# Attention of a two-block transformer kernel: heads handled one at a time, and in pairs that share the array

## The chip, the cores and the metric

The kernel runs on one core of a Trainium2 chip. The metric is the device time of one execution in microseconds. Before the change it is 2275.27 us, the median of three runs (2274.09 to 2283.27 us). The profile shown below is of a further execution of the same program.

## The reference

One sequence of 512 tokens, 1024 features wide, goes through two transformer blocks in float32. The change touches only the attention of the first one. All its heads have 64 features (`HEAD_DIM`), and a query attends to keys at or before it.

```
# first block, 8 NSA heads in 2 groups of 4, 8 DSA heads on one key head
s = einsum('bgrqd,bsgd->bgrqs', qb, kk) * scale       # window and selected branch: a key head per group
p = masked_softmax(s, mask); o = einsum('bgrqs,bsgd->bgrqd', p, vv)
o = g[..., 0:1] * o_cmp + g[..., 1:2] * o_slc + g[..., 2:3] * o_win
# DSA: the 128 best keys of each query by an index score, then the same softmax attention
score = where(key_pos <= tq, einsum('bqh,bqhs->bqs', w, relu(logits)), -inf); _, sel = top_k(score, 128)
o = concatenate([o_nsa, o_dsa], -1) @ w_out;  x = x + gt1 * rms_norm(o, g_post_mix)
```

At 512 tokens all selected blocks and the whole window lie within reach, so the selected and the window branch are plain causal attention with keys of their own. The compressed branch attends to 31 keys, each made from 32 tokens by a small two-layer network.

## The kernel before, in words

Everything is laid out with features on the partitions and tokens along the row. Each engine has one instruction stream, written out by hand, and semaphores tie the streams together. Nothing plans them: the order in the code is the order on the engine. `claim(bank, sem, value)` makes TensorE wait until the last reader of a PSUM bank is done.

The first block computes 16 projection tiles, then the attention in question, then the `w_out` product and the feed-forward layers. The second block follows. The attention is a loop over 96 jobs, `jobs = [(t, br, hh)]` (L268): `t` is one of four tiles of 128 queries, `br` is the branch (0 selected, 1 window, 2 DSA) and `hh` the head. A job of tile `t` sees `kv = (t+1) * 128` keys. Its steps are

- `qk` (L468), TensorE: scores into bank `j % 3`. A head has 64 features, so this matmul uses 64 of the 128 rows of the array.
- `masked` (L1392), VectorE: adds the mask to the negated scores, writes `sneg` in SBUF and takes the row's minimum.
- `Exp` (L986), ScalarE: from `sneg` into `prob`, with the row's sum.
- `scaled` (L1402), VectorE: reciprocal of the sum, then `prob` times it and the gate.
- `turn_probs` (L477), TensorE: `t+1` transposes of 128x128 into bank 3 or 4; `probs_turned` (L969), ScalarE: copies them to `probT`.
- `pv` (L485), TensorE: `t+1` matmuls, 64 columns of the array wide, into half of the partitions of bank 5 (NSA) or 6 (DSA).

In step `j` TensorE issues `qk(j)`, `turn_probs(j-2)` and `pv(j-3)`; VectorE `masked(j)` and `scaled(j-1)`; ScalarE the `Exp` of `j` and the copy of `j-2`. Other work is put between the jobs. TensorE has `ada_cols(2)` at job 2, `compress(0)` and `compress(1)` (L425, 32 matmuls each over weights that arrive in three tiles of the four-slot ring) at jobs 5 and 9, and `cmp_keys` at 14. The compressed branch of each tile has `cmp_scores` (L501), four jobs later `cmp_turn`, and seven jobs later `cmp_out`, which adds into bank 5. They use bank 7. VectorE has the 32 remaining rounds of the top-128 search (`top_round`, L1342: a `MAX8` and a match-replace over 384 or 512 scores), `late_mods`, its part of the compressed branch, and `outputs` (L1416), which splits a finished output bank into high and low parts for `w_out`. It also makes the low part of the first three `w_out` tiles (L1229) at job 31.

A float32 matmul shows as two records of TensorE in the trace, a transpose as one.

Of the kernel before, what the change touches and what calls it, by code (L numbers as in the profile page):

```python
# [10 lines left out]
ALU = mybir.AluOpType  # L11
# [3 lines left out]
P = 128  # L15
T = 512
# [120 lines left out]
def build(nc, xt, consts, cols, pos, ada, ada_late, mats, extra, out):  # L137
    ctx = ExitStack()
    with ctx:
# [38 lines left out]
        smin, _ = at("smin", [P, 3])  # L178
# [89 lines left out]
        jobs = [(t, br, hh) for t in range(NT) for br in range(3) for hh in range(HEADS)]  # L268
# [3 lines left out]
        CMP_AT = [16] + [24 * t for t in range(1, NT)]  # L272
# [13 lines left out]
        def _(pe):  # L286
# [181 lines left out]
            def qk(j):  # L468
                t, br, hh = jobs[j]
                kv = (t + 1) * P  # L470
                b = 64 * (hh // 4) if br < 2 else 64 * (hh % 2)
                q = QN + hh % 4 if br < 2 else QD + hh // 2
                claim(j % 3, "smin", j + 1)
                pe.matmul(bank[:, j % 3, 0:kv], proj[b:b + DH, q, t * P:(t + 1) * P],  # L474
                          proj[b:b + DH, (KSL, KW, KDD)[br], 0:kv], start=True, stop=True).then_inc(S("scores"), 1)

            def turn_probs(j):  # L477
                pe.wait_ge(S("probs_scaled"), j + 1)
                claim(3 + j % 2, "probT", j + 1)
                for i in range(jobs[j][0] + 1):  # L480
                    mm = pe.transpose(bank[:, 3 + j % 2, i * P:(i + 1) * P], prob[j % 4][:, i * P:(i + 1) * P],  # L481
                                      const("ident"))
                mm.then_inc(S("probs_turned"), 1)

            def pv(j):  # L485
                t, br, hh = jobs[j]
                vc = ((hh // 4) * DH, P + (hh // 4) * DH, 2 * P)[br]
                pe.wait_ge(S("probT"), j + 1)

                half = br // 2  # L490
                if hh == 0 and br != 1:
                    claim(5 + half, "oT", 2 * t + half + 1)
                b, c = DH * (hh % 2), hh // 2
                for i in range(t + 1):

                    mm = pe.matmul(bank[b:b + DH, 5 + half, c * P:(c + 1) * P], vtok[:, i, vc:vc + DH],  # L496
                                   probT[j % 4][:, i * P:(i + 1) * P], start=(i == 0 and hh < 2 and br != 1),
                                   stop=False, skip_group_check=True)
                mm.then_inc(S("pv"), 1)
# [22 lines left out]
            def cmp_out(t):  # L522
                pe.wait_ge(S("cmp_probT"), t + 1)
                for g in range(2):
                    for c in range(2):
                        pe.matmul(bank[:, 5, (2 * g + c) * P:(2 * g + c + 1) * P], vcmp[:, g, c * P:(c + 1) * P],
                                  cpt[:, g, :], start=False, stop=False, skip_group_check=True)

            pe.wait_ge(S("roped"), 16)
            n = len(jobs)  # L530
            for j in range(n + 3):
                if j < n:
                    qk(j)
                    if j == 2:
# [5 lines left out]
                    if j == 14:  # L540
                        cmp_keys()
                    if j in CMP_AT:
                        if j == CMP_AT[0]:
                            pe.wait_ge(S("cmp_kv"), 1)
                        cmp_scores(CMP_AT.index(j))
                    if j - 4 in CMP_AT:
                        cmp_turn(CMP_AT.index(j - 4))
                    if j - 7 in CMP_AT:
                        cmp_out(CMP_AT.index(j - 7))
                if 2 <= j < n + 2:  # L550
                    turn_probs(j - 2)
                if 3 <= j:
                    pv(j - 3)
# [299 lines left out]
        def _(act):  # L853
# [115 lines left out]
            def probs_turned(j):  # L969
                kv = (jobs[j][0] + 1) * P  # L970
                act.wait_ge(S("probs_turned"), j + 1)
                if j >= 4:
                    act.wait_ge(S("pv"), j - 3)
                act.activation(probT[j % 4][:, 0:kv], bank[:, 3 + j % 2, 0:kv], ACT.Copy).then_inc(S("probT"), 1)

            def outputs(t, half):
                act.wait_ge(S("pv"), 24 * t + 16 + 8 * half)
# [3 lines left out]
            for j, (t, br, hh) in enumerate(jobs):  # L981
                kv = (t + 1) * P
                act.wait_ge(S("smin"), j + 1)
                if j >= 4:
                    act.wait_ge(S("probs_turned"), j - 3)
                act.activation(prob[j % 4][:, 0:kv], sneg[j % 3][:, 0:kv], ACT.Exp, scale=-1.0,  # L986
                               bias=smin[:, j % 3:j % 3 + 1], accum_out=ssum[:, j % 4:j % 4 + 1])\
                   .then_inc(S("probs"), 1)
                if j in CMP_AT:
# [910 lines left out]
```

## Time and profile before

| | us |
|---|---|
| median of three runs | 2275.27 |
| the profiled execution, whole | 2262.76 |
| its span, first to last instruction | 2261.0 |
| TensorE matmul busy in the span | 2118.5 (94%) |
| TensorE weight load busy | 1613.5 (71%) |
| VectorE busy | 974.3 (43%) |
| ScalarE busy | 709.2 (31%) |

Busy time is time in which an instruction of that engine was running. The weight loads run beside the matmuls. The mean granted TensorE clock was 0.942 of full speed. The attention loop lies at 194 to 474 us of the span.

### The profile page before, as it was taken

The numbers are of one execution on the slowest core, as the hardware profiler recorded it, in microseconds if no ns is written. First come the engines' busy times: TensorE is split into PE (matmuls) and PEld (weight loads), VectorE is DVE, ScalarE is ACT, GpSimd is POOL, SyncE is SP. The second block draws the span as 40 slices with busy tenths as digits, with TensorE's granted clock in tenths as the row PEclk, the third lists the DMA queues.
The fourth block names the chain that finished last, engine by engine and source line by source line (L and its number), as shares of the span: only waits on it lengthen the run. The fifth ranks groups of instructions, "written<-read, shape, count | busy, mean of one in ns | idle before, by whom it ended". The sixth has DMA issues, their size and how long they took to land. (4 is left out here: it accounts for less than half of the span.)

```text
span 2261.0 us, 25224 instructions
## 1 busy us (share of the span) xinstructions
PE 2118.5 (94%) x10170; PEld 1613.5 (71%) x10170; DVE 974.3 (43%) x1654; ACT 709.2 (31%) x1163; POOL 124.7 (6%) x94
## 2 busy tenths in 40 slices
PE   5999999998999999999999989995898889999999
PEld 3666655575888887688888766663777767888887
DVE  4454587536443444533233423337544454332332
ACT  3321244434232333322223244546111133321221
POOL 0002000010000001000000102332000001000000
PEclk9997568999999999999999999997999999999999
DMA  8542000011222222123223121110000012232231
GB/s 334 186 158 105 28 29 1 1 47 56 94 95 97 97 94 93 56 99 107 84 93 121 57 75 57 47 38 0 1 1 1 2 56 84 93 115 75 99 118 50
DMA packets 41587, 172.14 MB, mean 76 GB/s; under 512 B 4609, under 2 KB 4865, under 8 KB 38145
## 3 DMA queue, kind: packets, MB, share of 16 engines
q1 hardware_dynamic: 41472, 170.54, 21.8%
q8 instruction: 81, 1.33, 0.2%
q14 instruction: 34, 0.27, 0.0%
HBM read 168.43 MB, written 2.10 MB: 75 GB/s over the span
## 5 line engine op out<-in xcount | busy, mean ns | idle before, releaser
L312 PE MATMUL bank<-hs,wsp 128*128 128x512 f32 x1392 | 554.0, 398 | 20.7 <-DVE hs L1268 11.5
L313 PE MATMUL bank<-hs,wsp 128*128 128x512 f32 x1392 | 545.9, 392 | 0.0
L314 PE MATMUL bank<-hs,wsp 128*128 128x512 f32 x1392 | 545.6, 392 | 0.0
L878 ACT ACTIVATE wsp<-ring 128x1024 fp32r<-128x1024 f32 (+2 forms) x244 | 268.8, 1104 | 851.8 <-PE bank L314 850.4
L1229 DVE TENSOR_TENSOR wsp<-ring,wsp 128x1024 fp32r<-128x1024 f32 (+2 forms) x244 | 312.0, 1281 | 383.2 <-ACT wsp L878 382.7
L312 PEld LDWEIGHTS bank<-hs,wsp 128*128 128x128 f32 x1392 | 263.9, 190 | 100.5 <-issue 38.7
L313 PEld LDWEIGHTS bank<-hs,wsp 128*128 128x128 f32 x1392 | 264.2, 190 | 55.7 <-issue 1.9
L314 PEld LDWEIGHTS bank<-hs,wsp 128*128 128x128 f32 x1392 | 263.8, 189 | 55.7
L314 PE MATMUL bank<-hids,wsp 128*128 128x512 f32 x608 | 241.0, 396 | 0.0
L313 PE MATMUL bank<-hids,wsp 128*128 128x512 f32 x608 | 241.0, 396 | 0.0
L312 PE MATMUL bank<-hids,wsp 128*128 128x512 f32 x608 | 241.0, 396 | 0.0
L313 PEld LDWEIGHTS bank<-hids,wsp 128*128 128x128 f32 x608 | 114.5, 188 | 27.9
L314 PEld LDWEIGHTS bank<-hids,wsp 128*128 128x128 f32 x608 | 114.5, 188 | 27.9
L312 PEld LDWEIGHTS bank<-hids,wsp 128*128 128x128 f32 x608 | 114.5, 188 | 27.9
L1739 POOL TENSOR_TENSOR arena<-arena 128x512 f32<-128x512 f32 x24 | 43.2, 1799 | 1382.2 <-ACT arena L890 1382.2
L1537 DVE SCALAR_TENSOR_TENSOR x<-bank,x 128x512 f32<-128x512 f32 x40 | 27.7, 692 | 174.8 <-PE bank L314 174.8
L474 PE MATMUL bank<-arena 64*128 64x128 f32 (+3 forms) x192 | 96.4, 594 | 3.0 <-DVE arena L1320 3.0
L986 ACT ACTIVATE arena<-arena,smin 128x128 f32<-128x128 f32 (+3 forms) x96 | 53.9, 561 | 128.8 <-DVE smin L1399 128.4
L496 PE MATMUL bank<-tmp,arena 128*64 128x128 f32 x480 | 88.9, 325 | 0.0
L1527 DVE TENSOR_TENSOR tmp<-tmp,bank 128x512 f32<-128x512 f32 x44 | 30.3, 688 | 128.5 <-PE bank L314 128.5
L496 PEld LDWEIGHTS bank<-tmp,arena 128*64 128x64 f32 x480 | 59.2, 159 | 20.8 <-issue 18.3
L481 PEld LDWEIGHTS bank<-cst,arena 128*128 128x128 f32 x240 | 30.0, 159 | 52.7 <-issue 32.4
(276 smaller groups left out, 2213.5 us busy)
## 6 DMA issues: line engine op xcount, KB each, us to landing
ring<-m_gate SPq DMA_DIRECT2D x44, 512.0 KB, 3.3
ring<-m_up SPq DMA_DIRECT2D x44, 512.0 KB, 3.3
ring<-m_down SPq DMA_DIRECT2D x32, 704.0 KB, 4.0
ring<-m_w_in SPq DMA_DIRECT2D x38, 512.0 KB, 3.4
arena<-ada_late SPq DMA_DIRECT2D x16, 1024.0 KB, 4.8
ring<-m_w_up SPq DMA_DIRECT2D x32, 512.0 KB, 3.3
ring<-m_w_down SPq DMA_DIRECT2D x32, 512.0 KB, 3.2
ring<-m_w_out SPq DMA_DIRECT2D x16, 512.0 KB, 3.4
```

Source lines behind the costliest of these rows:

```text
L312: pe.matmul(out, lhs[0], rhs[0], start=start, stop=False)
L313: pe.matmul(out, lhs[0], rhs[1], start=False, stop=False)
L314: return pe.matmul(out, lhs[1], rhs[0], start=False, stop=stop)
L474: pe.matmul(bank[:, j % 3, 0:kv], proj[b:b + DH, q, t * P:(t + 1) * P], proj[b:b + DH, (KSL, KW, KDD)[br], 0:kv], start=True, stop=True).t ...
L481: mm = pe.transpose(bank[:, 3 + j % 2, i * P:(i + 1) * P], prob[j % 4][:, i * P:(i + 1) * P], const("ident"))
L496: mm = pe.matmul(bank[b:b + DH, 5 + half, c * P:(c + 1) * P], vtok[:, i, vc:vc + DH], probT[j % 4][:, i * P:(i + 1) * P], start=(i == 0 an ...
L878: act.activation(wsp[:, s % SPLIT, 0, 0:size], ring[:, i % RING, 0:size], ACT.Copy)\
L986: act.activation(prob[j % 4][:, 0:kv], sneg[j % 3][:, 0:kv], ACT.Exp, scale=-1.0, bias=smin[:, j % 3:j % 3 + 1], accum_out=ssum[:, j % 4:j ...
L1229: dve.tensor_tensor(wsp[:, s % SPLIT, 1, 0:size], ring[:, i % RING, 0:size], wsp[:, s % SPLIT, 0, 0:size].bitcast(F32), ALU.subtract).then ...
L1527: dve.tensor_tensor(f, f, bank[:, 2 * (nn % 2) + 1, :], ALU.mult).then_inc(S("gated"), 1)
L1537: dve.scalar_tensor_tensor(out=x[:, nn, :], in0=bank[:, nn % 4, :], scalar=scale, in1=x[:, nn, :], op0=ALU.mult, op1=ALU.add).then_inc(S(" ...
L1739: pool.tensor_tensor(sq[:, 0, :], sq[:, 0, :], sq[:, k, :], ALU.add).then_inc(S("sq_sum"), 1)
```

## The change

The 96 jobs become 48 pairs of heads, `pairs = [(t, br, i)]`. The two heads of a pair lie in different row halves of the array for `qk` (partitions 0 to 63 and 64 to 127 of `proj`) and in different column halves for `pv`. For the NSA branches a pair is head `i` and head `i + 4`, one of each group; for DSA heads `2i` and `2i + 1`. Each step now issues both heads' `qk`, into two of four score banks, then both heads' transposes, then the `pv` matmuls alternately. Transposed probabilities go to banks 4 and 7, one bank for both heads while `t < 2` and one bank each after. `sneg` and `prob` are replaced by five pair buffers `soft`, in which mask, `Exp` and scaling work in place. One reciprocal serves both heads. The other work is put at the pair that corresponds to its old job or close to it, and the top-128 rounds go one to a pair from pair 4 to pair 35. The rows of `w_out` are reordered on the host to match.

```diff
-        sneg = [area(at * K, (T,)) for at in (66, 68, 70)]
-        prob = [area(at * K, (T,)) for at in (10, 12, 14, 16)]
-        probT = [tmp[:, at, :] for at in (2, 3, 4, 5)]
+        soft = [area(at * K, (2, T)) for at in (66, 70, 0, 10, 14)]
+        probT = [tmp[:, 2 + 2 * n:4 + 2 * n, :] for n in range(2)]
...
+        pairs = [(t, br, i) for t in range(NT) for br in range(3) for i in range(4)]
+        NP = len(pairs)
+        turned_at = list(itertools.accumulate(1 if t < 2 else 2 for t, br, i in pairs))
...
-        CMP_AT = [16] + [24 * t for t in range(1, NT)]
+        CMP_AT = [8] + [12 * t for t in range(1, NT)]
+        CMP_OUT_AT = [11] + [12 * t + 4 for t in range(1, NT)]
...
+            def qk(p):
+                t, br, i = pairs[p]
                 kv = (t + 1) * P
+                for e in range(2):
+                    b = 2 * (p % 2) + e
+                    claim(b, "smin", 2 * p + e + 1)
+                    pe.matmul(bank[:, b, 0:kv], proj[DH * e:DH * e + DH, (QN, QN, QD)[br] + i, t * P:(t + 1) * P],
+                              proj[DH * e:DH * e + DH, (KSL, KW, KDD)[br], 0:kv], start=True, stop=True)\
+                      .then_inc(S("scores"), 1)
+            def turn_probs(p):
+                t = pairs[p][0]
+                for e in range(2):
+                    if t < 2:
+                        b, c = (4, 7)[p % 2], 2 * e
...
+                    else:
+                        b, c = (4, 7)[e], 0
+                        claim(b, "probT", turned_at[p] - 1 + e)
+                    pe.wait_ge(S("probs_scaled"), 2 * p + e + 1)
+                    for k in range(t + 1):
+                        mm = pe.transpose(bank[:, b, (c + k) * P:(c + k + 1) * P], soft[p % 5][:, e, k * P:(k + 1) * P],
+                                          const("ident"))
...
+            def pv(p):
...
+                for k in range(t + 1):
+                    for e in range(2):
+                        vc = (e * DH, P + e * DH, 2 * P)[br]
+                        mm = pe.matmul(bank[DH * e:DH * e + DH, 5 + half, i * P:(i + 1) * P], vtok[:, k, vc:vc + DH],
+                                       probT[p % 2][:, e, k * P:(k + 1) * P], start=(k == 0 and i == 0 and br != 1),
+                                       stop=False, skip_group_check=True)
...
-                    if j == 5:
+                    if p == 2:
                         compress(0)
-                    if j == 9:
+                    if p == 4:
                         compress(1)
...
+            def probs_turned(p):                      # ScalarE
...
+                if p >= 2:
+                    act.wait_ge(S("pv"), p - 1)
+                if t < 2:
+                    act.wait_ge(S("probs_turned"), turned_at[p])
+                    act.activation(probT[p % 2][:, :, 0:kv],
+                                   bank[:, (4, 7)[p % 2], :].rearrange("p (e k) -> p e k", e=2)[:, :, 0:kv],
+                                   ACT.Copy).then_inc(S("probT"), 1)
...
+            def masked(p, e):                         # VectorE
...
+                if p >= 5:
+                    dve.wait_ge(S("probs_turned"), turned_at[p - 5])
...
+            def scaled(p):
+                t, br, i = pairs[p]
+                n = 2 * (p % 2)
+                dve.wait_ge(S("probs"), 2 * p + 2)
+                do(dve.reciprocal(rsum[:, n:n + 2], ssum[:, n:n + 2]))
+                for e in range(2):
+                    v, r = soft[p % 5][:, e, 0:(t + 1) * P], rsum[:, n + e:n + e + 1]
...
+            for p in range(NP + 1):
+                if p < NP:
+                    masked(p, 0)
+                    masked(p, 1)
...
+                if p >= 1:
+                    scaled(p - 1)
...
-                if rounds < 3 * ROUNDS and j < n and j >= (8, 8, 24)[rounds // ROUNDS] + 2 * (rounds % ROUNDS):
+                if rounds < 3 * ROUNDS and p >= 4 + rounds - ROUNDS:
                     top_round(rounds)
...
+    w_out = f["w_out"][0]
+    paired = w_out[0:512].reshape(2, 4, DH, D).transpose(1, 0, 2, 3).reshape(512, D)
```

## Rows read from the trace of the kernel before

**Rows 1.** Windows, tiles 0 to 3: busy PE, PEld, DVE, ACT, POOL, PEclk, DMA share, GB/s.

```profile
194.00:271.00 77.00, 73.20 (x293) 55.86 (x294) 32.05 (x142) 18.91 (x74) 0.00 (x0) 0.52 0.13 47
271.00:334.00 63.00, 60.35 (x212) 34.98 (x212) 50.76 (x162) 25.70 (x80) 0.00 (x0) 0.64 0.08 26
334.00:398.00 64.00, 63.80 (x285) 38.01 (x284) 42.33 (x133) 27.16 (x76) 0.00 (x0) 0.82 0.00 1
398.00:474.00 76.00, 74.53 (x387) 45.31 (x386) 37.58 (x111) 34.48 (x79) 0.00 (x0) 0.93 0.00 1
```

**Rows 2.** Waits at 194 to 474 us: waiter, releaser, us in total, times, longest.

```profile
DVE arena L1399 <- PE bank L474: 83.2, 49, 14.6
...
DVE arena L1427 <- PE bank L505: 10.4, 4, 3.2
```

**Rows 3.** Timeline of TensorE, one job of tile 3: start, us, line, records.

```profile
441.81 1.12 PE L474 MATMUL bank<-arena 64*128 64x512 f32 x2
442.86 0.66 PE L481 MATMUL bank<-cst,arena 128*128 128x128 f32 x4
443.45 1.09 PE L496 MATMUL bank<-tmp,arena 128*64 128x128 f32 x8
444.47 0.69 PE L474 MATMUL bank<-arena 64*128 64x512 f32 x1
```

**Rows 4.** Timeline of TensorE, one job of tile 1 at the low clock.

```profile
320.09 1.22 PE L474 MATMUL bank<-arena 64*128 64x256 f32 x2
321.24 0.69 PE L481 MATMUL bank<-cst,arena 128*128 128x128 f32 x2
321.86 1.12 PE L496 MATMUL bank<-tmp,arena 128*64 128x128 f32 x4
322.90 1.22 PE L474 MATMUL bank<-arena 64*128 64x256 f32 x2
```

**Rows 5.** Timeline of TensorE at 103.2 to 103.3 us, two index heads.

```profile
103.24 0.49 PE L422 MATMUL bank<-arena 64*128 64x256 f32 x2
```

**Rows 6.** Timeline of TensorE at 103.8 to 104.8 us, four column tiles of 32.

```profile
103.87 1.06 PE L374 MATMUL bank<-arena,c 128*32 128x512 f32 x8
```

**Rows 7.** Timeline of TensorE, `qk` of one job of tile 1, full clock.

```profile
304.31 0.70 PE L474 MATMUL bank<-arena 64*128 64x256 f32 x2
304.94 0.44 PE L481 MATMUL bank<-cst,arena 128*128 128x128 f32 x2
```

**Rows 8.** Timeline of TensorE in the second block, column halves, full clock.

```profile
1735.98 0.45 PE L792 MATMUL bank<-arena,wal 128*64 128x128 f32 x4
1736.25 0.40 PE L794 MATMUL bank<-arena 128*64 128x128 f32 x4
```

**Rows 9.** VectorE's groups by shape, 194 to 474 us: busy us, mean ns, idle before.

```profile
L1399 DVE CUSTOM_DVE_ANT_0 arena<-bank,cst 128x512 f32<-128x512 f32 x16 | 11.1, 691 | 20.5 <-PE bank L474 20.5
...
L1411 DVE TENSOR_SCALAR arena<-arena,rsum,gates 128x512 f32<-128x512 f32 x16 | 8.7, 547 | 0.6
...
L1399 DVE CUSTOM_DVE_ANT_0 arena<-bank,cst 128x128 f32<-128x128 f32 x24 | 6.9, 291 | 36.5 <-PE bank L474 35.7 <-DVE arena L1347 0.4
...
L1411 DVE TENSOR_SCALAR arena<-arena,rsum,gates 128x128 f32<-128x128 f32 x16 | 5.5, 346 | 0.6
```

**Rows 10.** VectorE's groups, shapes together, the same stretch.

```profile
L1346 DVE MAX8 best<-arena 128x8 f32<-128x384 f32 (+1 forms) x32 | 19.9, 620 | 0.0
L1347 DVE MATCH_REPLACE8 arena<-best,arena 128x384 f32<-128x384 f32 (+1 forms) x32 | 19.5, 609 | 0.0
L1408 DVE RECIPROCAL rsum<-ssum 128x1 f32<-128x1 f32 x96 | 15.3, 159 | 1.2 <-ACT arena L986 0.6
```

**Rows 11.** TensorE's groups, the same stretch.

```profile
L432 PE MATMUL bank<-wal,ring 128*128 128x64 f32 x128 | 27.8, 422 | 0.0
```

**Rows 12.** The page's costliest groups, whole span.

```profile
L1229 DVE TENSOR_TENSOR wsp<-ring,wsp 128x1024 fp32r<-128x1024 f32 (+2 forms) x244 | 312.0, 1281 | 383.2 <-ACT wsp L878 382.7
```

**Rows 13.** DMA issues at 160 to 300 us: KB each, us to landing.

```profile
ring<-m_cmp1v SPq DMA_DIRECT2D x3, 704.0 KB, 5.3
```

More of the change, by code:

```diff
@@ L1 @@
+import itertools
 from contextlib import ExitStack
@@ L466, in _ @@
             late_piece(15)
-            def qk(j):
-                t, br, hh = jobs[j]
+            def qk(p):
+                t, br, i = pairs[p]
                 kv = (t + 1) * P
[L471 to L475, printed above, removed]
@@ L490, in pv @@
+            def pv(p):
+                t, br, i = pairs[p]
                 half = br // 2
-                if hh == 0 and br != 1:
+                pe.wait_ge(S("probT"), turned_at[p])
+                if i == 0 and br != 1:
                     claim(5 + half, "oT", 2 * t + half + 1)
[L493 to L498, printed above, removed]
+                for k in range(t + 1):
[4 more added lines that the diff above has]
+                                       stop=False, skip_group_check=True)
@@ L967, in _ @@
             copy_ada_rows(2)
[L969 to L974, printed above, removed]
+            def probs_turned(p):
+                t = pairs[p][0]
+                kv = (t + 1) * P
+                if p >= 2:
[5 more added lines that the diff above has]
+                                   ACT.Copy).then_inc(S("probT"), 1)
+                else:
+                    for e in range(2):
+                        act.wait_ge(S("probs_turned"), turned_at[p] - 1 + e)
+                        act.activation(probT[p % 2][:, e, 0:kv], bank[:, (4, 7)[e], 0:kv], ACT.Copy)\
+                           .then_inc(S("probT"), 1)
@@ L976, in outputs @@
             def outputs(t, half):
-                act.wait_ge(S("pv"), 24 * t + 16 + 8 * half)
+                act.wait_ge(S("pv"), 9 if t + half == 0 else 12 * t + 8 + 4 * half)
                 act.activation(hs[:, 0, 4 * half:4 * half + 4, t * P:(t + 1) * P],
                                bank[:, 5 + half, :].rearrange("p (c t) -> p c t", c=4), ACT.Copy).then_inc(S("oT_hi"), 1)
-            for j, (t, br, hh) in enumerate(jobs):
+            for p, (t, br, i) in enumerate(pairs):
                 kv = (t + 1) * P
[L983 to L989, printed above, removed]
-                    act.wait_ge(S("cmp_shift"), CMP_AT.index(j) + 1)
+                for e in range(2):
+                    n = 2 * (p % 2) + e
+                    act.wait_ge(S("smin"), 2 * p + e + 1)
+                    act.activation(soft[p % 5][:, e, 0:kv], soft[p % 5][:, e, 0:kv], ACT.Exp, scale=-1.0,
+                                   bias=smin[:, n:n + 1], accum_out=ssum[:, n:n + 1]).then_inc(S("probs"), 1)
+                if p in CMP_AT:
+                    act.wait_ge(S("cmp_shift"), CMP_AT.index(p) + 1)
@@ L1845, in lay_out @@
         mats["cmp1" + name] = np.ascontiguousarray(w1.reshape(P, 3, SLOT).transpose(1, 0, 2))
-    mats["w_out"] = tiles(f["w_out"][0])
+    w_out = f["w_out"][0]
+    paired = w_out[0:512].reshape(2, 4, DH, D).transpose(1, 0, 2, 3).reshape(512, D)
+    mats["w_out"] = tiles(np.concatenate([paired, w_out[512:]], 0))
     mats["w_up"] = tiles(f["w_up"][0])
```

146 lines of the change are left out of this document (64 added, 82 removed).

## The prediction, made before the change was run

> **What bounds the kernel now.** Busy shares of a whole span mix stages, so I began with the windows and cut the attention loop, 194 to 474 us, at its four query tiles. The matmul records of TensorE fill 272 of 280 us, VectorE is busy 163 and ScalarE 106 [rows 1]. The table of waits says the same from the other side: VectorE waited 83 us for scores [rows 2]. So TensorE sets the pace, and the loop can shrink only as far as TensorE's work does and VectorE lets it.
>
> Two things are to be seen in the rows of TensorE. First, the granted clock: 0.52, 0.64, 0.82 and 0.93 of full over the four tiles [rows 1]. The clock has two levels, 2.4 and 1.2 GHz, so (1 - share) x 2 of each window passed at the lower: 74, 45, 23 and 11 us, about 153 of the 280. Second, the make-up of a job. In tile 3 at full clock scores, transposes and `pv` start at 441.81, 442.86 and 443.45, and the next job at 444.47 [rows 3]: 1.05, 0.59 and 1.02 us, 2.66 together. Four more records of 128 columns make the difference between 0.59 and 1.02, so one pass of 128 columns costs 0.108 us. The job has 8 + 4 + 8 passes, 2.16 us; 0.50 us is lost at its three changes of kind. Tile 1 at the lower clock: 1.15, 0.62, 1.04, together 2.81 [rows 4]; a pass is 0.21 us (two more passes cost 0.42), the job has 4 + 2 + 4, so 2.1 us and 0.71 fixed. By the passes (5, 10, 15, 20 for tiles 0 to 3) a job costs 1.76, 2.81, 3.86, 4.91 us at the lower clock and 1.04, 1.58, 2.12, 2.66 at full; the 1.58 appears as such, from 302 to 306 us, of which the `qk` part of 0.63 is shown [rows 7].
>
> **The change, part by part.** *Do the halves of the array run together?* All hangs on it, and the trace has both kinds. Two index heads in the two row halves start both their first records within 0.1 us, two records by 103.3 [rows 5], and the whole pair over 256 keys, four records, is done when the next line starts at 103.87 [rows 6], 0.63 us. One head of tile 1 over 256 keys takes 304.31 to 304.94, also 0.63 [rows 7]. The second head was free. Column tiles: eight records of four tiles of 32 columns take 1.06 us [rows 6], where one 512-column matmul takes 1.05 [rows 3]. And two heads in the column halves with 128 rows, the very form of `pv`: four records from 1735.98 to 1736.25, 0.27 us [rows 8], where already two passes one after the other cost 0.22. So `qk` and `pv` of a pair cost what one head's do now, and the transposes, which use the whole array, double.
>
> The Trainium skill says otherwise on one point. TensorE: Matmul & The Clock Gate, Part 3 (The mechanism) has it that matmuls are "pc-monotone in start AND end — strict FIFO, no reordering". If each head's two records are issued together, by that rule the second head could not start until the first head's second record did, and a pair would cost one and a half times a head. The trace disagrees: the second record is there within 0.1 us, not after 0.3. It stands as a rival below.
>
> *TensorE per pair*: a job plus t+1 passes. At the lower clock 1.97, 3.23, 4.5, 5.75 us for tiles 0 to 3; at full clock 1.15, 1.8, 2.44, 3.09. Two jobs now: 5.32 in tile 3 at full clock, 4.24 in tile 2, 5.62 in tile 1 at the lower, 3.5 in tile 0.
>
> *VectorE per pair*: the mask step 291 to 691 ns and the scaling 346 to 547 by width, evenly spaced in between (133 and 67 ns for 128 columns) [rows 9], twice each, and one reciprocal of 159 instead of two [rows 10]: 1.44, 1.83, 2.24, 2.64 us, and some 0.15 for handing over between instructions (an estimate from starts in the timeline). The search adds one round per pair at pairs 4 to 35: 620 + 609 ns and gaps [rows 10], 1.3 us. With it: 2.9 in tile 0, 3.3 in tile 1, 3.8 to 3.9 in tile 2 (its rounds are the wide ones); 2.8 without it in tile 3. So VectorE takes over as the bound from pair 4 to somewhere in tile 2. The half of the reciprocals that goes saves 48 x 0.16 = 7.6 us of an engine that sets the pace in most of the loop; it is inside these sums. ScalarE has 34.5 us in tile 3 for 24 jobs [rows 1], 2.9 a pair, under TensorE's 3.09, and its copies for tiles 0 and 1 become one for two heads.
>
> *Depth and waits.* What is queued behind each new wait: on TensorE `turn_probs(p-2)` waits for `scaled(p-2)`, and behind it are `pv(p-3)` and `qk(p+1)`. In tile 3 counted from the start of `qk(p-1)`: scores at 1.15, two mask steps to 2.55, scaling of pair p-2 to 3.8; TensorE asks for it at 3.09 + 1.05. `pv(p-3)` needs the copies behind the two `Exp` of p-1, at about 4.6, and asks at 3.09 + 2.1. There is slack of 0.3 to 0.6 us, so the five buffers are never the limit in steady state; I count 0.06 us a pair for it, 3.15.
>
> *Moved steps.* `compress(1)` comes two pairs after `compress(0)`, 3.3 us by the prices above, where four jobs gave 7. Its last two weight tiles can only be fetched into slots that `compress(0)` frees, and land 5.3 us after issue [rows 13]: the cover is gone and TensorE waits some 2.5 us there. `cmp_scores` and its relatives keep their count. They share bank 7 with the transposes, so each tile gets a chain of scores, mask, turn and copy through that bank. VectorE waits 10.4 us in four times for `cmp_scores` already [rows 2]; with its nine short operations a tile the branch costs about 7 us a tile when VectorE is the bound. I take 7 (bounds 4, if it all lies beside TensorE, and 10). The host's reordering of `w_out` and the splits at pair 15 and 16 cost what they did, three of 1.28 us [rows 12].
>
> **The sum**, tile by tile, against 194.0 to 473.8 us of the trace, 279.8 us.
> - Tile 0, now 77.4 (271.5 less 194.0): pairs 0 to 3 at 2.0 = 8; 128 records of `compress` are 27.8 us busy at the lower clock [rows 11] and stay, 27.4; eight pairs at 2.9 = 23; the weight wait 2.5; VectorE's nine copies for the compressed keys 2.5; the branch 7; the start with `ada_cols` 1.5. Together 72.
> - Tile 1, now 62.7: TensorE 3.23 at the lower clock and VectorE 3.3 lie so close that neither covers the other's slips, 3.35 x 12 = 40; branch 7; outputs with their waits 4; `w_out` splits 3.8. Together 55.
> - Tile 2, now 63.5: VectorE alone would give 3.9, TensorE at the lower clock 4.5, at full 2.44. The present loop shows both levels in this tile [rows 1] and I expect both again, as a full-clock TensorE would stand idle 1.5 of 3.9 us and a low one not at all. 4.2 x 12 = 50; 7; 4. Together 61.
> - Tile 3, now 76.1: the search is over, TensorE is the bound at full clock: eleven steps of 3.15 = 35; 9 for the first steps (the same tile now loses 9 over eight times 2.66 there); 1 for outputs; 9 to drain three pairs and the last output. Together 54.
>
> 72 + 55 + 61 + 54 = 242, 38 us less. The profiled execution was 2262.8 us and would be 2225; the median of the runs, 12.5 us above it, goes from 2275.3 to 2237. Nothing else of the program is touched, and the `w_out` product starts behind the last output as now.
>
> **The rivals.**
> 1. *The clock stays low through tiles 2 and 3.* For it: TensorE will have idle time in tile 2 that it has not now, and low spells of 23 and 11 us are there already. Against: in tile 3 a pair at the lower clock leaves TensorE no idle time at all, and the present jobs came back from just that state. Tile 2 at 4.5 gives 65, tile 3 at 5.75 with its longer drain 90: 72 + 55 + 65 + 90 = 282, and 2277 us.
> 2. *A pair costs one and a half heads* in `qk` and `pv`. At tile 3 that adds half of 16 passes, 0.86 us, 10 us over the tile; 0.64 at full clock in tile 2, partly under VectorE, 5; 0.84 at the lower in tile 1, 9; 1 in tile 0: 25 of the 38 go, 2262 us.
> 3. *VectorE's queue and TensorE's waits add instead of overlapping*, as masks wait for scores queued behind a `pv` that waits for ScalarE. At 0.7 us a pair in tiles 1 and 2 and 0.4 in tile 3: 22 us, 2259 us. For it: 83 us of such waits now. Against: `qk` may run two pairs ahead.
> 4. *Each change of half drains the array.* Then the halves don't overlap and the alternating `pv` pays at every matmul the 0.17 us that a change of kind costs now. In tile 3 eight such changes for two, 1.0 us above two jobs, or with `qk`'s 1.2; 0.8 in tile 2, 0.5 in tile 1, 0.2 in tile 0: 12 x 2.7 = 32 us slower, 2307 us. It decides if the second half's record starts after its partner ends. The skill's TensorEngine Tiling (Array Packing), Key Properties, lets only a change of mode drain and not of tile, and here the rows side with it: four records in 0.27 us [rows 8] leave no room for a drain between them.
>
> **Chances.** Forecast 0.70, rival 3 0.12, rival 1 0.08, rival 4 0.05, rival 2 0.05. A change of 0.5%, 11 us, is about what a measurement can tell. Faster by more: the forecast, rival 3 and half of rival 2, 0.85. Within: rival 1 and half of rival 2, 0.10. Slower: rival 4, 0.05. Low end: VectorE's pace in tiles 1 and 2 with TensorE at full clock (3.3 and 3.9 a pair, 4 us less), the branch at 4 a tile (12 less), drain and start shorter (9 less): 2212. High end: past rivals 2 and 3, short of rival 1, 2268.
>
> **What would show it.** Two records of L474's successor starting together, in both the score and the `pv` lines; a pair every 3.1 us in tile 3; VectorE busy 155 to 160 us in a loop of some 242, hardly waiting for TensorE from pair 5 to tile 2; a wait of a few us before the second `compress`; the clock at its lower level in tiles 0 and 1. The forecast fails if the pair in tile 3 takes over 4 us, or if PEclk of tile 3 falls under 0.8.

## The result: 2208.22 us, faster by more than forecast

The changed kernel takes 2208.22 us (median of four runs, 2207.65 to 2210.44), beside 2274.79 for the kernel before (median of four): a ratio of 0.9701, interval 0.9677 to 0.9725. That is 66.6 us less. The forecast was 2237, 38 us less, with a range from 2212, so the direction was right and the time lies 4 us below the range. The profiled execution took 2208.48 us, its span is 2206.7 (2261.0 before).

The page of the changed kernel, whole span:

```profile
span 2206.7 us, 25046 instructions
...
PE 2030.2 (92%) x10202; PEld 1568.1 (71%) x10202; DVE 963.1 (44%) x1606; ACT 704.1 (32%) x1139; POOL 124.7 (6%) x94
...
PEclk9997589999999999999999999996999989999999
```

TensorE lost 88 us of busy time, VectorE 11. The windows of the changed kernel, tiles 0 to 3 and then two stretches of the rest, with the columns of [rows 1]:

```profile
194.00:260.50 66.50, 57.03 (x294) 47.05 (x294) 28.10 (x128) 16.78 (x62) 0.00 (x0) 0.50 0.14 54
260.50:304.00 43.50, 30.84 (x212) 18.90 (x210) 38.36 (x126) 21.89 (x63) 0.00 (x0) 0.75 0.11 37
304.00:354.00 50.00, 37.38 (x282) 23.17 (x280) 44.76 (x133) 25.33 (x72) 0.00 (x0) 0.90 0.00 1
354.00:412.50 58.50, 50.20 (x428) 33.99 (x424) 39.93 (x115) 36.12 (x86) 0.00 (x0) 0.91 0.01 2
412.80:1500.00 1087.20, 1041.83 (x4334) 808.07 (x4334) 426.11 (x533) 388.02 (x562) 99.45 (x74) 0.98 0.23 78
1500.00:2206.00 706.00, 647.97 (x3906) 530.85 (x3906) 286.85 (x404) 160.09 (x217) 10.17 (x6) 0.95 0.17 56
```

In tile 2 TensorE is busy 37 of 50 us and VectorE 45, in tile 1 31 and 38 of 43.5: there VectorE looks like the bound now, and e5 and e4 below test it. In tile 3 TensorE still is, 50 of 58.5. The last two lines are the rest of the program. Before, the stretch of the same 3906 matmuls took 700 us:

```profile
1561.00:2261.00 700.00, 640.92 (x3906) 526.27 (x3906) 286.72 (x404) 159.81 (x216) 10.17 (x6) 0.96 0.17 56
```

The waits of the changed kernel in the loop (columns as in [rows 2]):

```profile
ACT arena L1010 <- DVE smin L1422: 75.8, 46, 3.6
...
DVE arena L1422 <- PE bank L481: 22.3, 12, 11.5
...
DVE arena L1422 <- issue: 16.2, 1, 16.2
```

VectorE waited 83.2 us for scores in [rows 2] and waits 22.3 now, and 16.2 more in one wait beside the second `compress` for which the profile names no releaser. ScalarE's waits for VectorE, the largest here, were larger before:

```profile
ACT arena L986 <- DVE smin L1399: 128.4, 87, 3.8
```

TensorE's timeline in tile 3, one pair, the counterpart of [rows 3]:

```profile
387.07 1.13 PE L481 MATMUL bank<-arena 64*128 64x512 f32 x4
388.13 1.09 PE L497 MATMUL bank<-cst,arena 128*128 128x128 f32 x8
389.15 1.09 PE L512 MATMUL bank<-tmp,arena 128*64 128x128 f32 x16
390.17 1.13 PE L481 MATMUL bank<-arena 64*128 64x512 f32 x4
```

Four score records take 1.06 us where two took 1.05, sixteen of `pv` 1.02 where eight did. Only the transposes take longer (0.59 to 1.02), as there are twice as many. Two heads every 3.11 us (387.07 to 390.17, the mean of six such steps), where one head took 2.66.

### The profile page after: what moved, and what is told of

Read it like the earlier page. It is cut to its first block and busy times, and to the rows that moved or that the text cites. A ratio compares the mean times of both kernels' runs of the same rounds, so it can differ in the third digit from the quotient of the medians.

```text
span 2206.7 us, 25046 instructions
## 1 busy us (share of the span) xinstructions
PE 2030.2 (92%) x10202; PEld 1568.1 (71%) x10202; DVE 963.1 (44%) x1606; ACT 704.1 (32%) x1139; POOL 124.7 (6%) x94
## 5 line engine op out<-in xcount | busy, mean ns | idle before, releaser
L1563 DVE SCALAR_TENSOR_TENSOR x<-bank,x 128x512 f32<-128x512 f32 x40 | 27.7, 692 | 174.6 <-PE bank L321 174.6
L497 PE MATMUL bank<-cst,arena 128*128 128x128 f32 x240 | 45.0, 325 | 23.6 <-ACT tmp L997 7.7
L1196 ACT ACTIVATE wal<-bank 128x512 f32<-128x512 f32 x40 | 23.9, 598 | 117.5 <-PE bank L774 117.5
L786 PE MATMUL bank<-arena,wal 128*128 128x128 f32 x320 | 43.2, 278 | 8.6 <-DVE arena L1696 8.6
```

What stands on the lines that cost most here:

```text
L497: mm = pe.transpose(bank[:, b, (c + k) * P:(c + k + 1) * P], soft[p % 5][:, e, k * P:(k + 1) * P], const("ident"))
L786: mm = pe.matmul(bank[:, 5, i * P:(i + 1) * P], powT(i), Z[:, i, :], start=True, stop=True)
L1563: dve.scalar_tensor_tensor(out=x[:, nn, :], in0=bank[:, nn % 4, :], scalar=scale, in1=x[:, nn, :], op0=ALU.mult, op1=ALU.add).then_inc(S(" ...
```

## The experiments

Ratios are to the kernel before, run on the same chip. Differences in us between versions are of their medians; by the ratios they would come out up to 2 us otherwise. "Loop" is the time from the first `qk` record to the first record of the `w_out` product, "rest" the span less the loop, both from the trace; the four tiles start at their first `qk`. "Low" is the time that TensorE's clock spent at its lower level in each tile.

| kernel | median us | tiles 0, 1, 2, 3 | loop | rest | low |
|---|---|---|---|---|---|
| before, as shown | 2274.79 | 77.4, 62.7, 63.5, 76.2 | 279.8 | 1981.2 | 75, 46, 23, 10 |
| before again (e0) | 2273.59 | 78.7, 72.8, 63.4, 79.3 | 294.2 | 1979.6 | 79, 73, 22, 17 |
| after | 2208.22 | 66.4, 43.6, 50.3, 58.3 | 218.6 | 1988.1 | 66, 21, 10, 10 |
| e1 same rows | 2224.76 | 67.9, 51.7, 54.4, 63.1 | 237.2 | 1988.4 | 67, 45, 31, 7 |
| e2 `pv` grouped | 2212.77 | 66.5, 45.3, 51.9, 62.7 | 226.4 | 1987.8 | 67, 29, 17, 10 |
| e3 three deep | 2209.73 | 66.6, 43.8, 50.0, 57.7 | 218.1 | 1989.8 | 67, 22, 10, 10 |
| e5 rounds moved | 2194.74 | 66.8, 44.9, 37.4, 57.0 | 206.2 | 1987.0 | 66, 33, 3, 10 |
| e6 branch off bank 7 | 2201.32 | 66.5, 43.5, 49.1, 52.9 | 212.0 | 1987.7 | 67, 21, 17, 3 |
| e8 no overlap | 2233.27 | 70.4, 44.4, 58.9, 69.0 | 242.7 | 1989.1 | 70, 21, 17, 0 |
| e4 no rounds | 2181.01 | 64.5, 32.7, 37.3, 57.2 | 191.7 | 1987.4 | 65, 14, 3, 10 |
| e9 before, rounds moved | 2273.50 | 82.1, 52.9, 59.8, 80.9 | 275.7 | 1979.9 | 82, 27, 14, 21 |
| e7 e5 and e6 together | 2178.95 | 65.5, 41.1, 34.3, 49.9 | 190.9 | 1987.3 | 66, 26, 0, 0 |
| e10 with unread matmuls | 2178.00 | 64.1, 41.4, 34.3, 51.4 | 191.3 | 1986.0 | 52, 30, 0, 3 |
| e11 the same, spread | 2182.11 | 56.4, 45.2, 37.7, 51.4 | 190.7 | 1986.2 | 44, 21, 3, 3 |

**Do the row halves overlap?** e1 puts both heads of a pair on the same rows.

```diff
-                    pe.matmul(bank[:, b, 0:kv], proj[DH * e:DH * e + DH, (QN, QN, QD)[br] + i, t * P:(t + 1) * P],
-                              proj[DH * e:DH * e + DH, (KSL, KW, KDD)[br], 0:kv], start=True, stop=True)\
+                    pe.matmul(bank[:, b, 0:kv], proj[0:DH, (QN, QN, QD)[br] + i, t * P:(t + 1) * P],
+                              proj[0:DH, (KSL, KW, KDD)[br], 0:kv], start=True, stop=True)\
```

> The changed kernel, but both heads' score matmuls read row half 0 (the second head's scores are those of the first, so this output is another). All else is as in the change, so only the overlap of the row halves is undone. Theory A (the halves overlap, TensorE is the bound in tile 3, VectorE in tiles 0 to 2): a pair in tile 3 goes from 3.11 to about 3.97 us, eight more passes of 0.108; in tiles 1 and 2 most of the 0.43 and 0.65 us hides under VectorE's 2.8 and 3.45; the start of each tile gains a little. 10 to 14 us slower than the change, 2218 to 2223. Rival B (the gain came from fewer waits and the deeper buffers, not from the halves): within 3 us of 2208.

Measured: 2224.76 us (2223.98 to 2227.3), ratio 0.9769 (0.9745 to 0.9792), 16.5 us above the change and 2 above the expected range. TensorE in tile 3:

```profile
420.48 1.98 PE L481 MATMUL bank<-arena 64*128 64x512 f32 x4
422.39 1.09 PE L497 MATMUL bank<-cst,arena 128*128 128x128 f32 x8
423.41 1.09 PE L512 MATMUL bank<-tmp,arena 128*64 128x128 f32 x16
```

The four score records take 1.91 us, not 1.06: the second head costs 0.85 when it has no half of its own. The steps of tile 3 are 3.96 us, 0.85 more. Of the 18.6 us that the loop lost, 8 lie in tile 1 (51.7 for 43.6), where the clock stayed low for 45 us instead of 21. At the lower level the four score records take 2.01 us there (301.62 to 303.63), and the last four steps 4.10 us each, over VectorE's pace:

```profile
301.62 2.07 PE L481 MATMUL bank<-arena 64*128 64x256 f32 x4
303.63 1.11 PE L497 MATMUL bank<-cst,arena 128*128 128x128 f32 x4
```

So the 16.5 us are the lost overlap together with a lower clock.

**Does the order of `pv` matter?** e2 issues all chunks of one head, then all of the other.

```diff
-                for k in range(t + 1):
-                    for e in range(2):
+                for e in range(2):
+                    for k in range(t + 1):
```

> The changed kernel with the loops of pv exchanged: all key blocks of the first head, then all of the second, instead of alternating. Same matmuls, same column halves. Theory A1 (TensorE runs the two halves side by side whatever the order of issue, as the records of lines 792 and 794 of the kernel before hint): no change, 2207 to 2210. Theory A2 (the halves overlap only between neighbours in the order of issue): the pv part of a pair in tile 3 grows by seven or eight passes of 0.108, 0.8 us, and tile 3 by 10; 2217 to 2221.

Measured: 2212.77 us (2210.43 to 2215.96), ratio 0.9711 (0.9683 to 0.9738): 4.5 us above the change, with intervals that overlap, and between the two expected ranges. The steps in the trace are plain. TensorE in tile 3:

```profile
398.50 1.09 PE L497 MATMUL bank<-cst,arena 128*128 128x128 f32 x8
399.53 1.58 PE L512 MATMUL bank<-tmp,arena 128*64 128x128 f32 x16
401.04 0.70 PE L481 MATMUL bank<-arena 64*128 64x512 f32 x2
```

`pv` takes 1.51 us, between 1.02 (alternating) and the 1.89 of e8 (no halves). The second head's first record begins 0.49 us after the first head's, when five of the first head's eight have started. Neither full overlap nor strict order holds, as if TensorE looked ahead over a few instructions only; what sets the five is not shown. So the alternation in the change is worth 0.48 us a pair at this width; `qk`, with two records a head, needs none.

**How much does the depth do?** e3 keeps three buffers of `soft` of five.

```diff
...
-                if p >= 5:
-                    dve.wait_ge(S("probs_turned"), turned_at[p - 5])
+                if p >= 3:
+                    dve.wait_ge(S("probs_turned"), turned_at[p - 3])
...
-                dve.tensor_tensor_reduce(soft[p % 5][:, e, 0:kv], bank[:, n, 0:kv], mask, 1.0, 3e38, ALU.add, ALU.min,
+                dve.tensor_tensor_reduce(soft[p % 3][:, e, 0:kv], bank[:, n, 0:kv], mask, 1.0, 3e38, ALU.add, ALU.min,
```

> The changed kernel with three pair buffers in place of five: soft[p % 3], and the mask step waits for the transposes of pair p-3 instead of p-5. On TensorE those transposes stand before qk(p) in the same stream, and the mask step waits for qk(p) anyway. Theory A (the depth does nothing here): 2207 to 2211. Rival B (the depth pays, as it lets VectorE run ahead): slower by 3 us or more, 2211 and up.

Measured: 2209.73 us (2207.54 to 2210.61), ratio 0.9699 (0.9676 to 0.9722), with the same steps, 3.45 and 3.11 us. The depth of five gives nothing over three.

**How much is the overlap, and how much the pairing alone?** e8 keeps the pairs, their order and their buffers, and takes both halves away: `qk` as in e1, and both heads of a pair in the same columns in `pv`.

```diff
-                        mm = pe.matmul(bank[DH * e:DH * e + DH, 5 + half, i * P:(i + 1) * P], vtok[:, k, vc:vc + DH],
-                                       probT[p % 2][:, e, k * P:(k + 1) * P], start=(k == 0 and i == 0 and br != 1),
+                        mm = pe.matmul(bank[DH * (i % 2):DH * (i % 2) + DH, 5 + half, i * P:(i + 1) * P], vtok[:, k, vc:vc + DH],
+                                       probT[p % 2][:, e, k * P:(k + 1) * P], start=(k == 0 and i < 2 and e == 0 and br != 1),
```

> The changed kernel with neither overlap: both heads' score matmuls use row half 0, and both heads' pv one column half (the half alternates from pair to pair). Scores of second heads and all outputs are others than the reference's; numbers and sizes of the instructions are the same. Theory A (the overlap is nearly the whole gain): TensorE's pair in tile 3 is 2 jobs less one set of changes, 5.32 - 0.50 = 4.8 us; in tile 2 at full clock 3.7, in tile 1 at the lower 4.9 or 2.7 at full; the loop takes 255 to 275 us, the kernel 2245 to 2265. Rival B (the gain is in the pairing of the other steps): under 2235.

Measured: 2233.27 us (2232.83 to 2233.88), ratio 0.9812 (0.9777 to 0.9847), the time of Rival B. TensorE in tile 3:

```profile
419.74 1.98 PE L481 MATMUL bank<-arena 64*128 64x512 f32 x4
421.65 1.09 PE L497 MATMUL bank<-cst,arena 128*128 128x128 f32 x8
422.67 1.96 PE L512 MATMUL bank<-tmp,arena 128*64 128x128 f32 x16
424.56 0.69 PE L481 MATMUL bank<-arena 64*128 64x512 f32 x1
```

A pair takes 4.83 us here, 3.74 in tile 2 and 2.66 in tile 1: each is two jobs of before (5.32, 4.24, 3.16) less 0.5. That fits changes of kind paid once for two heads instead of twice; over 48 pairs it is 24 us at full clock. Tile 1 went from 72.8 us (e0) to 44.4, with 21 us at the lower clock for 73. So without any overlap the kernel is already some 41 us faster than before (the interval gives 35 to 51), and the overlap of halves adds 25. The overlap, on which I said all hangs, is the smaller part. How the other 17 of the 41 us divide between the clock, the work that was moved and the single reciprocal is not shown.

By the medians the rows are worth 16.5 of the 25 us (e1), which leaves 8.5 for the columns, but that split is not clean: e1 ran tile 1 at the lower clock for 45 us, and this run, with more work for TensorE, for 21. By the steps of tile 3, all at full clock, the two halves are worth the same: 0.85 us a pair for the rows (3.11 to 3.96) and 0.87 for the columns (3.96 to 4.83).

**Is it VectorE that holds tile 2?** e5 takes search rounds out of tiles 1 and 2: 19 of the 32 rounds of VectorE are put at pairs 2 and 4, where it waits while TensorE does `compress`.

```diff
-                if rounds < 3 * ROUNDS and p >= 4 + rounds - ROUNDS:
+                for _ in range({2: 9, 4: 10}.get(p, 1 if 5 <= p < 18 else 0)):
```

> The changed kernel with the 32 rounds of the top-128 search moved: 9 at pair 2 and 10 at pair 4, beside the two compress blocks of 13.7 us in which VectorE now has nothing to do, and one each at pairs 5 to 17. The same work, the same result. Theory A (VectorE is the bound from pair 5 into tile 2): tile 2 loses its 12 rounds of 1.4 us and goes from 3.45 a pair towards TensorE's 2.44 at full clock, half of tile 1 from 2.9 to between 1.9 and 3.2 by the clock; 12 to 22 us faster than the change, 2186 to 2196. Rival C (TensorE or its clock is the bound there): less than 5 us, 2203 to 2209.

Measured: 2194.74 us (2192.87 to 2195.23), ratio 0.9633 (0.9611 to 0.9656), 13.5 us below the change and within the expected range, nearly all of it in tile 2 (50.3 to 37.4). TensorE in tile 2:

```profile
333.70 0.92 PE L481 MATMUL bank<-arena 64*128 64x384 f32 x4
334.55 0.90 PE L497 MATMUL bank<-cst,arena 128*128 128x128 f32 x6
335.38 0.88 PE L512 MATMUL bank<-tmp,arena 128*64 128x128 f32 x12
336.19 0.92 PE L481 MATMUL bank<-arena 64*128 64x384 f32 x4
```

The step falls from 3.45 us to 2.46 and 2.49 in turn, close to the forecast's price of TensorE for this tile (2.44). e4 leaves the 32 rounds of the loop out altogether:

```diff
-                if rounds < 3 * ROUNDS and p >= 4 + rounds - ROUNDS:
-                    top_round(rounds)
-                    rounds += 1
```

> The changed kernel without the 32 rounds of the search in the loop, so the masks of tiles 2 and 3 are raw scores and the output is another. Theory A (VectorE is the bound of tiles 0 to 2 only through the rounds): pairs at TensorE's price, 2.44 in tile 2 and 1.8 at full clock in tile 1; as the moved rounds of e5 without its last 13, 2185 to 2192. Rival (TensorE's waits for ScalarE and VectorE take over): no better than e5, 2194.

Measured: 2181.01 us (2177.32 to 2181.12), ratio 0.9583 (0.9551 to 0.9615), 4 us under the expected range. TensorE in tile 1:

```profile
286.16 0.70 PE L481 MATMUL bank<-arena 64*128 64x256 f32 x4
...
287.97 0.70 PE L481 MATMUL bank<-arena 64*128 64x256 f32 x4
```

The last steps of tile 1 take 1.81 us, TensorE's price again (1.8), so VectorE holds tile 1 as well as tile 2. The 27 us are what the search costs in this loop.

The same move in the kernel before, where TensorE is the bound, is e9:

```diff
-                if rounds < 3 * ROUNDS and j < n and j >= (8, 8, 24)[rounds // ROUNDS] + 2 * (rounds % ROUNDS):
+                for _ in range({5: 9, 9: 10}.get(j, 1 if 10 <= j < 23 else 0)):
```

> The kernel before, one head at a time, with the search rounds moved beside the compress blocks: 9 at job 5, 10 at job 9, one each at jobs 10 to 22. The same move took 14 us from the changed kernel. Theory A (there VectorE is the bound, here TensorE is): within 4 us of the kernel before. Rival C (the rounds cost as much here): 10 to 15 us faster.

Measured: 2273.50 us beside 2272.47, ratio 0.9999 (0.9958 to 1.004). Its ten runs fall into two groups, five of 2257.35 to 2264.75 us and five of 2282.24 to 2289.23, so the median stands for neither, and an effect of less than 9 us can't be excluded. An effect of 13.5 us, what the same edit is worth after the change, lies outside the interval: the change moved the bound.

**Was the shown profile of before a typical execution?** e0 is the kernel before, unchanged, profiled again.

> The kernel before, unchanged, to see a second execution of it in the trace. Its shown profile took 2262.8 us, 12 us less than its runs, while the changed kernel's profile took just what its runs take; the changed kernel's program after the attention loop lasted 1794 us in the trace and the same code before 1787. Theory A (the shown profile caught a short execution): this one takes 2270 to 2280, with the attention loop at 280 and some 6 to 12 us more elsewhere, in low spells of the clock. Rival B (the change speeds or slows what follows it): the rest lasts 1787 again.

Measured: 2273.59 us, ratio 0.998 (0.9955 to 1.0004), and this profiled execution took 2275.59, near the median, where the shown one took 2262.76. I had expected the extra time outside the loop; it is inside. Its four tiles:

```profile
193.00:271.50 78.50, 74.93 (x294) 57.24 (x294) 32.11 (x142) 19.34 (x74) 0.00 (x0) 0.50 0.13 46
271.50:344.30 72.80, 71.67 (x211) 40.55 (x210) 51.05 (x162) 25.56 (x79) 0.00 (x0) 0.50 0.07 22
344.30:407.70 63.40, 62.92 (x283) 37.55 (x282) 42.14 (x133) 26.73 (x73) 0.00 (x0) 0.83 0.00 1
407.70:487.00 79.30, 77.87 (x388) 47.25 (x386) 37.67 (x112) 34.98 (x81) 0.00 (x0) 0.89 0.00 1
```

Tile 1 ran at 1.2 GHz from end to end (0.50), the sixteen jobs behind its first eight at 2.81 us; in the shown execution the clock rose within it (0.64 in [rows 1], the jobs of 1.58 us in [rows 7]). The 13 us between the two profiled executions are in the loop, 294.2 against 279.8 us, and the rest is alike. With that rest, a run at the median would have a loop of about 293 us; that is worked out, as only these two executions were profiled.

**What sharing bank 7 costs.** The scores and turned probabilities of the compressed branch share bank 7 with the transposes. e6 moves them to bank 6, which is free while the first half's outputs gather in bank 5, and the branch starts four pairs later in tiles 1 to 3. So the run changes two things at once, the bank and the place.

```diff
-        CMP_AT = [8] + [12 * t for t in range(1, NT)]
-        CMP_OUT_AT = [11] + [12 * t + 4 for t in range(1, NT)]
+        CMP_AT = [8] + [12 * t + 4 for t in range(1, NT)]
+        CMP_OUT_AT = [11] + [12 * t + 8 for t in range(1, NT)]
...
-                claim(7, "cmp_masked", t + 1)
+                claim(6, "cmp_masked", t + 1)
...
```

> The changed kernel with the compressed branch moved from bank 7, which the transposes of odd or second heads now use as well, to bank 6, which lies idle from the last output of a tile to the DSA pairs of the next. For that its three steps come four pairs later in tiles 1 to 3. Same work, same result. In the changed kernel TensorE stood still about 3 us before the branch's scores in tiles 2 and 3, as bank 7 was to be copied by ScalarE first, and again at the branch's transposes. Theory A (the shared bank makes those stalls): 4 to 9 us faster, 2199 to 2204. Rival B (they are VectorE's queue or the late outputs of the tile before): within 2 us of 2208.

The wait that it aims at, in tile 3 of the changed kernel:

```profile
357.53 0.84 ACT L997 ACTIVATE tmp<-bank 128x384 f32<-128x384 f32 x2
...
358.43 0.74 PE L521 MATMUL bank<-arena 64*128 64x32 f32 x5 [2.88 <-ACT tmp L997]
```

The branch's scores waited 2.9 us for a copy out of the shared bank, and later a pair's transposes 1.3 for VectorE's copy of the branch out of it. Measured: 2201.32 us (2200.7 to 2201.81), ratio 0.9671 (0.9636 to 0.9706), 6.9 us below the change, 5.4 of it in tile 3. What of it is the bank and what the later start, no run separates.

**All of it together** is e7: e6, most rounds at the two `compress` steps, and the second `compress` one pair later, when its weights are there.

```diff
-                    if p == 4:
+                    if p == 5:
...
-                if rounds < 3 * ROUNDS and p >= 4 + rounds - ROUNDS:
+                for _ in range({2: 10, 5: 10}.get(p, 1 if p > 2 else 0) if rounds < 3 * ROUNDS and p < NP else 0):
```

> The changed kernel with three moves: 10 search rounds beside each compress block and the rest one to a pair by pair 15; the second compress block one pair later, so that its weights land beside pair work; the compressed branch in bank 6 as in the run beside it. If all three add up: 14 (measured for the rounds alone) + 2 + what bank 6 gives; 2183 to 2192. If bank 6 gives nothing: 2192 to 2195.

Measured: 2178.95 us (2177.4 to 2179.97), ratio 0.9572 (0.9538 to 0.9607), 29.3 us below the change and 4 under the expected range. Tiles 2 and 3:

```profile
300.00:334.00 34.00, 32.07 (x280) 20.39 (x278) 27.55 (x97) 25.18 (x73) 0.00 (x0) 1.00 0.01 1
334.00:384.60 50.60, 45.68 (x431) 30.88 (x430) 37.00 (x108) 35.58 (x86) 0.00 (x0) 1.00 0.01 2
```

TensorE is busy 32 of 34 and 46 of 51 us, and the clock is at full throughout. This and e10 are the fastest versions that leave no work out.

**Can the clock be kept up in tile 0?** e10 adds to e7 three matmuls ahead of the loop that nobody reads, in the idle stretch in front of it.

```diff
+            claim(0, "ropein", 16)
+            for _ in range(3):
+                pe.matmul(bank[:, 0, :], const("ones"), x[:, 0, :], start=True, stop=True)
```

> The run e7 with three float32 matmuls of 128x512 that nobody reads in the 3 us before the loop in which TensorE waits for the last rotated tile. The clock fell to its lower level at that place and stayed there for the 66 us of tile 0. Theory A (the idle gap brings the fall): the clock stays up into pair 0 to 2, and if the compress blocks then run at full clock too, they take 7 us instead of 14 each: 10 to 18 us faster than e7, 2161 to 2169. Rival B (the small matmuls of tile 0 and of compress bring it down wherever it starts): the fall comes 5 to 15 us later and 0 to 5 us are won.

Measured: 2178.00 us (2174.98 to 2179.06), ratio 0.9573 (0.9546 to 0.96), the same as e7, where 10 to 18 us were expected. The first `compress` step fell from 14.8 us to 7.8, and the time came back two pairs on, in a step of 9.9 us for 2.1. TensorE in tile 0:

```profile
204.26 0.49 PE L481 MATMUL bank<-arena 64*128 64x128 f32 x4
212.90 0.66 PE L497 MATMUL bank<-cst,arena 128*128 128x128 f32 x2 [8.14 <-DVE arena L1438]
```

The scaling waited for stood behind ten search rounds, now longer than the step that had covered them. e11 takes fewer of them:

```diff
+                for _ in range({2: 5, 5: 7}.get(p, 1 if p > 2 else 0) if rounds < 3 * ROUNDS and p < NP else 0):
```

> The run e10 with 5 search rounds at pair 2 and 7 at pair 5 instead of 10 and 10, the others one to a pair to pair 24. In e10 the unread matmuls kept the clock up over the first compress block, 7 us instead of 14, but VectorE's ten rounds of 1.25 us then outlasted it and TensorE stood still for 8 us. Theory A (that wait ate the gain): 3 to 8 us faster than e10 and e7, 2170 to 2176, and up to 8 more if the clock now stays up over the second block. Rival B (the eight rounds that move into tiles 1 and 2 cost what is won): 2176 to 2181.

Measured: 2182.11 us (2178.62 to 2183.98), ratio 0.9601 (0.9582 to 0.962). Tile 0 gained 8 us more (56.4), and tiles 1 and 2 gave back 3.8 and 3.4, with the remaining rounds in them. The loop is 190.7 us for 191.3, in a profiled execution (2178.62) that was the fastest of the four. No gain, and the median is above both expected ranges; why the loop stays at 191 us is open.

## Why the prediction was right in direction and wrong in size

The miss is 29 us, and its terms can be told apart by the forecast's own sum. The four tiles were to take 72, 55, 61 and 54 and took 66.4, 43.6, 50.3 and 58.3: 5.6, 11.4 and 10.7 less, 4.3 more, together 23.4 us (5.6 + 11.4 + 10.7 - 4.3). The offset between profile and median, 12.5 us, was carried over and isn't there any more. And the rest of the program, costed at nothing, took 6.9 us more. 23.4 + 12.5 - 6.9 = 29.0.

- *The halves run together*: right. `qk` and `pv` of a pair cost what one head's did, 1.06 and 1.02 us. Rivals 2 and 4 fall with that: the change doesn't pay the 0.85 us that the row halves save (e1), and without halves at all (e8) the kernel is still faster than before.
- *TensorE's price, a job plus t+1 passes*: right to 0.05 us where TensorE sets the pace. 3.11 for 3.09 in tile 3, 2.46 to 2.49 for 2.44 in tile 2 (e5), 1.81 for 1.8 in tile 1 (e4), 1.97 for 1.97 in tile 0.
- *VectorE takes over from tile 1*: the mechanism is right, the size is the first failed term. I summed the mean durations of single instructions and added 0.15 us for handing over. VectorE's timeline in tile 2 of the changed kernel, one pair:

```profile
340.18 0.56 DVE L1422 CUSTOM_DVE_ANT_0 arena<-bank,cst 128x384 f32<-128x384 f32 x1
...
340.67 0.55 DVE L1422 CUSTOM_DVE_ANT_0 arena<-bank,cst 128x384 f32<-128x384 f32 x1
...
341.15 0.16 DVE L1430 RECIPROCAL rsum<-ssum 128x2 f32<-128x2 f32 x1
341.34 0.87 DVE L1435 TENSOR_SCALAR arena<-arena,rsum,gates 128x384 f32<-128x384 f32 x2
342.13 0.69 DVE L1368 MAX8 best<-arena 128x8 f32<-128x512 f32 x1
...
343.64 0.56 DVE L1422 CUSTOM_DVE_ANT_0 arena<-bank,arena 128x384 f32<-128x384 f32 x1
```

  The second mask step starts 0.49 us after the first, which lasts 0.56; two scalings of 0.48 take 0.87; the next operation starts 0.08 us before they end. Everything but the search round takes 1.95 us (340.18 to 342.13) where I had 2.24 + 0.15; in tile 1 it is 1.55 for 1.98. That is 0.43 us a pair, 10 us over the two tiles. Where VectorE had nothing but a pair and its round, the pitch was 3.45 and 2.79 us, not 3.8 to 3.9 and 3.3.
- *The clock in tile 2*: the second failed term. "As a full-clock TensorE would stand idle 1.5 of 3.9 us and a low one not at all" I mixed both levels into 4.2 us a pair. Measured: full clock for 40 of the 50 us, steps of 3.45, with TensorE busy only 37. That is some 4 us more. In tile 1 I had the low level throughout and the trace has it for 21 of 43.5. In the second half of tile 2 TensorE stood idle for up to 0.88 us in every step and kept the full clock:

```profile
322.80:326.30 3.50, 3.50 (x18) 2.03 (x16) 2.41 (x6) 1.18 (x3) 0.00 (x0) 0.51 0.03 5
326.30:354.00 27.70, 22.05 (x202) 13.72 (x202) 25.61 (x79) 16.98 (x49) 0.00 (x0) 1.00 0.00 1
```

  The two low spells of this tile, from 309.2 and from 322.8 us, came behind waits of 3.17 and 2.59 us, and where the clock fell at the end of tile 3, TensorE had stood idle for 2.01 us:

```profile
401.58 1.09 PE L512 MATMUL bank<-tmp,arena 128*64 128x128 f32 x16
404.68 1.93 PE L497 MATMUL bank<-cst,arena 128*128 128x128 f32 x8 [2.01 <-ACT tmp L997]
```

- *The other steps of tiles 1 and 2*: twelve pitches of 2.79 and of 3.45 us leave 10.1 and 8.9 us for the branch, the outputs and the `w_out` splits, where the sum had 14.8 and 11. These terms were together 7 us too high; which of them, no run separates.
- *Tile 0*: of its 5.6 us, 3.9 lie in the first five steps, 38.4 us for the 42.3 that the sum gives them. The first two pairs took 3.1 us where pairs and start were to take 5.5.
- *Tile 3*: eleven steps in 45.1 us for 45 is right, though its base was misread: in the shown execution the first eight jobs of this tile lose 7 us over eight times 2.66, not 9. The drain behind the last `qk` is the error, 13.2 us for 9, with the last two pairs' transposes and `pv` partly at the low clock just seen (1.93 for 1.09).
- *The weight wait before the second `compress`*: 2.5 us predicted, 2.84 measured:

```profile
217.72 1.51 PE L439 MATMUL bank<-wal,ring 128*128 128x64 f32 x6 [2.84 <-DMA ring<-m_cmp1v]
```

- *Depth never the limit*: right, and more so than said; three buffers do (e3).
- *The branch at 7 us a tile*: not measured by itself. e6, with another bank and a later start, takes 5.4 us off tile 3, 1.2 off tile 2 and nothing off tile 1.
- *The offset of 12.5 us*: the third failed term. It was a stretch of low clock in tile 1 that the shown execution happened to lack (e0), inside the very loop that the change rewrites. Against the execution of e0 the loop went from 294.2 to 218.6 us, 75.6 less, and the rest took 8.5 more: 67, as the medians have it. Of the 75.6, tile 1 alone is 29.
- *"Nothing else of the program is touched"*: the fourth failed term, small. All ten versions built on the change have a rest of 1986 to 1990 us, the two profiled executions of the kernel before and the one of e9 have 1979.6 to 1981.2. The difference lies in the last stretch, 706 us for 700 with the same matmuls, and there in the second block's attention alone: counted from the first record of the `w_out` product, the same matmul records start within 0.2 us of the same time up to 1044 us, and 6.8 us later from 1400 us to the end. TensorE's clock is lower for longer after the loop, 116 us for 99, which could be worth up to 8 us. But e4 has 106 us of it and is nearly as much longer (5.9 us), so the clock needn't be the whole of it; the cause is open.

Of the rivals, the third (queues and waits add up) and the first (the clock stays low) are both refuted by tile 2: 3.45 us a pair is VectorE's own work and no more.

## What to carry to other kernels

Read a pair's or a job's pitch from consecutive starts in the timeline, not from a sum of durations: it is 0.43 us in 2.4 off here. Where profile and median differ by more than the scatter you care about, find where the profiled execution was short before carrying the difference over; it may lie in the stretch that is being changed. Packing two small heads into the halves of the array pays twice, once by overlap (25 us of 67) and once without it (41, of which fewer changes of kind make 24 by the steps at full clock; the rest isn't told apart); and after it the bound is elsewhere, so work of VectorE that showed no price before (e9: 0, within 9 us) has one (e5: 13.5 us).

## What was not expected of the hardware

- TensorE lets a second column half start early, but only when its records stand near: with eight records of the first head ahead of it the second began after about five, and `pv` took 1.51 us, between 1.02 and 1.89 (e2).
- VectorE starts an instruction some 0.08 us before the record of the last one ends, in the mask and scaling steps (0.49 for 0.56, 0.87 for two of 0.48).
- The kernel before, run again and again, scatters by 19 us (2265.39 to 2284.76 over 13 runs), the changed one by 3 (four runs); the profiled executions show the clock of tile 1 at 0.50 in one and 0.64 in another.
- With TensorE busy 22 of 27.7 us, in turns with up to 0.88 us of idle time between them, the granted clock was full (1.00).
